# Experts of a mixture layer taken in pairs: a new order of units, one turning for two experts, and another ending for the last block

## The reference

```python
grp = jnp.argmax(g_logits, axis=-1)                 # one of 8 groups per token
top_val, top_idx = lax.top_k(e_logits, TOP_K)       # 2 of the 8 experts of that group
comb = jax.nn.softmax(top_val, axis=-1) * p_grp
# for each expert e, on its tokens:
h = jax.nn.silu(xb @ w1[e]) * (xb @ w3[e])          # 1024 -> 256, twice
y = h @ w2[e]                                       # 256 -> 1024
```

## Time and profile before

| | us |
|---|---|
| median of 3 runs | 1932.17 (1927.52 to 1934.03) |
| the profiled execution | 1933.65 |
| its span, first to last instruction | 1931.8 |
| PE busy | 1886.8 (98%) |
| DVE busy | 1437.1 (74%) |
| ACT busy | 1217.5 (63%) |

### The profile page before, as it was taken

One profiled execution on the slowest core, in us unless ns is written; L12 is line 12 of the kernel. 1 busy time (PEld: TensorE's weight loads), 2 busy tenths in 40 slices (PEclk: granted clock), 3 DMA queues, 4 the chain that ended last, 5 costly groups with the idle time before them and its releaser, 6 DMA issues.

```text
span 1931.8 us, 27066 instructions
## 1 busy us (share of the span) xinstructions
PE 1886.8 (98%) x9252; PEld 1571.1 (81%) x9252; DVE 1437.1 (74%) x1838; ACT 1217.5 (63%) x1538; POOL 162.3 (8%) x169
## 2 busy tenths in 40 slices
PE   9999999999999999999899999999999999999997
PEld 7978878888888888888789788788888888888885
DVE  5455544589899899999834655454898999999897
ACT  5455544357777777777634655434677777777775
POOL 1000000220010011010000000002200110110000
PEclk9999999999999999999999999999999999999999
DMA  5221193499999999999612222925999999999992
GB/s 173 71 66 45 52 236 114 185 332 395 391 383 365 386 385 366 381 389 373 217 66 59 66 65 74 239 90 183 371 394 384 385 367 376 393 370 375 386 381 99
DMA packets 158791, 503.54 MB, mean 261 GB/s; under 512 B 22410, under 2 KB 38794, under 8 KB 158704
## 3 DMA queue, kind: packets, MB, share of 16 engines
q1 hardware_dynamic: 146192, 459.70, 64.2%
q0 software_dynamic: 12512, 42.69, 7.6%
HBM read 490.18 MB, written 32.79 MB: 271 GB/s over the span
## 4 chain that ended last, share of the span: by engine, by line
PE 87%; DVE 6%; issue 2%; ACT 2%; DMA 2%; DVEq 0%; POOL 0%; SPq 0%; ACTq 0%; POOLq 0%
PE ps L1639 25%; PE ps L1641 25%; PE ps L1640 24%; PE ps L1882 3%; DVE wl L1115 2%; PE ps L1818 2%; PE ps L1868 2%; DMA yb<-yrows 2%; PE ps L2012 1%; PE ps L1973 1%; PE ps L1927 1%; PE ps L1985 1%; PE ps L1686 1%; DVE gb L1398 1%; DVE wl L1120 1%
## 5 line engine op out<-in xcount | busy, mean ns | idle before, releaser
L1115 DVE TENSOR_TENSOR wl<-raw,wh 128x2048 fp32r<-128x2048 f32 (+1 forms) x402 | 908.5, 2280 | 154.1 <-ACT wh L717 151.8
L717 ACT ACTIVATE wh<-raw 128x2048 fp32r<-128x2048 f32 (+1 forms) x406 | 754.3, 1884 | 64.6 <-PE ps L1641 64.0
L1639 PE MATMUL ps<-wh,xgh 128*128 128x512 f32 x1024 | 412.5, 403 | 0.2
L1641 PE MATMUL ps<-wh,xgl 128*128 128x512 f32 x1024 | 400.2, 391 | 0.0
L1640 PE MATMUL ps<-wl,xgh 128*128 128x512 f32 x1024 | 399.2, 390 | 0.0
L1641 PEld LDWEIGHTS ps<-wh,xgl 128*128 128x128 f32 x1024 | 192.2, 188 | 41.8
L1639 PEld LDWEIGHTS ps<-wh,xgh 128*128 128x128 f32 x1024 | 192.3, 188 | 37.7 <-issue 2.4
L1640 PEld LDWEIGHTS ps<-wl,xgh 128*128 128x128 f32 x1024 | 192.9, 188 | 36.1
L1639 PE MATMUL ps<-wh,hth 128*128 128x512 f32 x512 | 200.2, 391 | 3.1 <-DVE htl L1170 3.1
L1641 PE MATMUL ps<-wh,htl 128*128 128x512 f32 x512 | 200.0, 391 | 0.0
L1640 PE MATMUL ps<-wl,hth 128*128 128x512 f32 x512 | 199.3, 389 | 0.0
(11 more groups left out here) (320 smaller groups left out, 2658.6 us busy)
## 6 DMA issues: line engine op xcount, KB each, us to landing
raw<-in_w SPq DMA_DIRECT2D x512, 512.0 KB, 6.2
raw<-in_w SPq DMA_DIRECT2D x128, 1024.0 KB
raw<-in_w_gate SPq DMA_DIRECT2D x16, 1024.0 KB
xslots<-zrow POOLq DMA_DIRECT2D x2, 6240.0 KB, 36.2
raw<-in_w_out SPq DMA_DIRECT2D x8, 1024.0 KB
xg<-xslots POOLq DMA_DIRECT2D x14, 520.0 KB, 7.2
raw<-in_w_in SPq DMA_DIRECT2D x8, 800.0 KB
raw<-in_w_oa SPq DMA_DIRECT2D x4, 1024.0 KB
```

Of the source, the lines that this page charges most:

```text
L717: return nc.scalar.activation(dst, src, ACT.Copy)
L1115: return V.tensor_tensor(dst, src, hi.bitcast(F32), ALU.subtract)
L1639: MM(dst, lh, rh, start=first, stop=False)
L1641: return MM(dst, ll, rh, start=False, stop=last)
```

## The change

The unit list goes by pairs of experts: four up halves (both experts of a pair), then the two downs of the pair before. The pair's turn follows the second of these downs: four transposes in a row into the two halves of `ps2`, one copy of 512 columns on ACT, one on DVE. The two last downs of a block stand after the four first units of the next block, and the turn of experts 0 and 1 behind them (in block 0, which has no such tails, it stands after up 2 half 0). `y_first` and `y_second` move with the tail of expert 7, four units later than before. The transposes of the next block's rows move behind down 3; those of `sel` move from up 3 to up 4. The adds of earlier rows move to the first up halves of experts 4, 5, 6 and 7. In the last block the last units are up 6, up 6, up 7, down 4, up 7 (turn of 6), down 5 (turn of 7), down 6, down 7.

```diff
-    FIRST = [("up", 0, 0), ("up", 0, 1)]
-    for e in range(1, NE):
-        FIRST.append(("up", e, 0))
-        if e >= 2:
-            FIRST.append(("down", e - 2, 0))
-        FIRST.append(("up", e, 1))
-    FIRST.append(("down", NE - 2, 0))
-    LAST = [("tail", NE - 1, 0)]
-    NEXT = FIRST[:1] + LAST + FIRST[1:]
...
+    FIRST, NEXT = ups(0), ups(0) + downs(NE - 2, "tail")
+    for e in range(2, NE, 2):
+        FIRST += ups(e) + downs(e - 2)
+        NEXT += ups(e) + downs(e - 2)
+    ENDING = [("up", NE - 2, 0), ("up", NE - 2, 1), ("up", NE - 1, 0), ("down", NE - 4, 0), ("up", NE - 1, 1),
+              ("down", NE - 3, 0)] + downs(NE - 2)
+    ALONE = FIRST[:-6] + ENDING
+    FINAL = NEXT[:-6] + ENDING
+
+    def turned_after(u, units):
+
+        kind, e, half = u
+        if kind == "tail":
+            return [0, 1] if e == NE - 1 else []
+        if u == ("up", 2, 0):
+            return [0, 1] if units[4] == u else []
+        if units[-1] == ("down", NE - 1, 0) and e >= NE - 3:
+            return {("up", NE - 1, 1): [NE - 2], ("down", NE - 3, 0): [NE - 1]}.get(u, [])
+        return [e + 1, e + 2] if kind == "down" and e % 2 else []
...
-                act.wait_ge(S["used_m"], b * NU + (NU + 1))
+                act.wait_ge(S["used_m"], b * NU + (NU + 4))
...
-                        if kind == "up" and 3 <= e < 3 + NT and half == 0 and prepared and not prepare:
-                            earlier_rows(e - 3)
+                        if kind == "up" and e >= NE - NT and half == 0 and prepared and not prepare:
+                            earlier_rows(e - (NE - NT))
...
+                    def turn(experts):
+                        pe.wait_ge(S["hw_done"], b * NE + (experts[-1] + 1 + BASE["hw_done"]))
+                        pe.wait_ge(S["htl_done"], b * NE + (experts[0] + BASE["htl_done"]))
+                        for e in experts:
+                            for j in range(FE // P):
+                                at = (e % 2 * (FE // P) + j) * P
+                                last = nc.tensor.transpose(ps[2][:, at:at + P], hw[:, e % 2, j * P:(j + 1) * P],
+                                                           ident[:, :])
+                        last.then_inc(S["ht_ps"], len(experts))
...
-                        if u == ("up", NE - 3, 1) and prepare:
+                        if u == ("down", NE - 5, 0) and prepare:
                             rows_turned(b + 1)
```

More of the change, by code:

```diff
@@ L109, in user_before, with ups, downs @@
         return max((k for k in range(n) if at[k] == at[n]), default=None)
-    FIRST = [("up", 0, 0), ("up", 0, 1)]
-    for e in range(1, NE):
-        FIRST.append(("up", e, 0))
-        if e >= 2:
-            FIRST.append(("down", e - 2, 0))
-        FIRST.append(("up", e, 1))
-    FIRST.append(("down", NE - 2, 0))
-    LAST = [("tail", NE - 1, 0)]
-    NEXT = FIRST[:1] + LAST + FIRST[1:]
-    turn_after = {("up", 1, 0): 0}
-    for e in range(1, NE):
-        turn_after["down", e - 1, 0] = e
+    def ups(e):
+        return [("up", x, half) for x in (e, e + 1) for half in range(2)]
+    def downs(e, kind="down"):
+        return [(kind, x, 0) for x in (e, e + 1)]
+    FIRST, NEXT = ups(0), ups(0) + downs(NE - 2, "tail")
[15 more added lines that the diff above has]
+        return [e + 1, e + 2] if kind == "down" and e % 2 else []
     ctx = ExitStack()
@@ L338, in hybrid_trunk, with hth_of, ht_of @@
         block = ctx.enter_context(nc.Block())
+        def hth_of(experts, part=hth):
+            return part[:, experts[0] % 2:experts[0] % 2 + len(experts), :, :].rearrange("p e k t -> p (e k t)")
+        def ht_of(experts):
+            at = experts[0] % 2 * FE
+            return ps[2][:, at:at + len(experts) * FE]
         def dist_of(t):
@@ L534, in load_units @@
                         else:
-                            ex = (tail_g if kind == "tail" and i < 2 else g) * NE + e
+                            ex = (tail_g if kind == "tail" else g) * NE + e
                             src = w2[l].rearrange("e (k p) n -> e p k n", p=P)
@@ L540, in _ @@
                 load_units(FIRST, ND, 0, 0, None)
-                with sp.Fori(0, NG - 1) as r:
+                with sp.Fori(0, NG - 2) as r:
                     load_units(NEXT, ND + len(FIRST), r, r + 1, r)
-                load_units(LAST, ND + len(FIRST) + len(NEXT), NG - 2, NG - 1, NG - 1)
-                n_blocks = overflow(sp, lambda b, g: load_units(FIRST + LAST, ND, b, g, None))
+                load_units(FINAL, ND + len(FIRST), NG - 2, NG - 1, NG - 2)
+                n_blocks = overflow(sp, lambda b, g: load_units(ALONE, ND, b, g, None))
                 if l < L - 1:
@@ L1007, in step @@
                         kind, e, half = u
[L1008 to L1012, removed]
+                        turned = turned_after(u, units)
+                        if turned:
+                            act.wait_ge(S["ht_ps"], b * NE + (turned[-1] + 1))
+                            nc.scalar.activation(hth_of(turned), ht_of(turned), ACT.Copy
+                                                 ).then_inc(S["hth_done"], len(turned))
                         if kind == "up" and half == 1:
@@ L1024, in step @@
                             nc.scalar.activation(selt[:, :], ps[7][:, :], ACT.Copy).then_inc(S["selt_done"], 1)
-                        if kind == "tail" and n < n0 + 2:
+                        if u == ("tail", NE - 1, 0):
                             y_first(b - 1)
@@ L1573, in step @@
                         kind, e, half = u
[L1574 to L1578, removed]
+                        turned = turned_after(u, units)
+                        if turned:
+                            dve.wait_ge(S["hth_done"], b * NE + (turned[-1] + 1))
+                            lo_part(hth_of(turned, htl), ht_of(turned), hth_of(turned)
+                                    ).then_inc(S["htl_done"], len(turned))
                         if kind == "up" and half == 1:
@@ L2033, in pe_block @@
                         else:
-                            down(n0 + i, e, kind == "down" or i >= 2)
+                            down(n0 + i, e, kind == "down")
                         if u == ("up", 0, 0) and isinstance(b, int) and b == 0:
@@ L2041, in pe_block @@
                             last.then_inc(S["slot_ps"], 1)
-                        if u in turn_after:
-                            turn(turn_after[u])
-                        if u == ("up", NE - 3, 1) and prepare:
+                        if turned_after(u, units):
+                            turn(turned_after(u, units))
+                        if u == ("down", NE - 5, 0) and prepare:
                             rows_turned(b + 1)
-                        if u == ("up", 3, 0) and not prepare:
+                        if u == ("up", 4, 0) and not prepare:
                             pe.wait_ge(S["sel_made"], (b - (NG - 2)) * NT)
```

6 lines of the change are left out of this document (3 added, 3 removed).

## The result

Side by side on the same chips, the changed kernel takes 1936.24 us (median of 19 runs, 1932.03 to 1938.51) and the kernel before 1932.37 us (19 runs, 1925.38 to 1934.21): ratio 1.0021, 95% interval 1.0013 to 1.0028. That is 4 us more, inside the 0.3% that the prediction counts as no change, and 3 us above its 1933.1. The time fell into the range; the sum behind it was right in its large terms, and missed one that gains and two that cost.

The account below looks back on a forecast made before the run. PE was taken to be bound by its own matmuls, so only transposes and waits could change. Terms -4.6 - 0.6 + 3.2 + 2.9 = +0.9 us on the median 1932.2 gave 1933.1; range 1927 to 1942.

Parts of the forecast that it names:

- turns (and tail): PE's transposes: one going-in less per pair, 76 x 0.06 = -4.6 us; waits at block-end tails gone, -0.6.
- the loop's branch: PE at the loop's end: the branch's cost was taken to stay, so no gain was counted.
- block 0: Turn of 0 and 1 waits for DVE's `hw` of expert 1: +1.6 us per layer, +3.2 in all.
- last block, DVE's wait: Second add waits for its load, so PE waits before turns of 4 and 5 and of 7: +2.9 us for both layers.
- clock at a layer's end: PE's granted clock at the last turn and downs: forecast to stay 1.00, costing nothing.
- The loop's own branch stays: Loop end: the tail's loss goes, but the branch's own cost on PE remains after the change.
- the load's wait: Last block: DVE loses 3.1 us at the second add, waiting for its load of earlier rows.
- its first rival: Long wait before the turn of 7 lowers PE's clock: some +3 us per layer; 1939, or 1945 with late load; chance 0.24.
- The rival's other half, a late fourth load: Last block: the fourth add's load takes 7.8 us, so the turn of 7 comes 2.9 us later.
- Wrong if the clock falls at the end of a layer: A sign that would refute the forecast: granted clock below 1.00 at a layer's end.
- no steady block has idle PE: Steady blocks: any idle PE there would show the forecast wrong; they were to be 0.3 us shorter.
- the turn of 4 and 5 waits: Last block: PE loses about 1.1 us before this turn; the forecast is wrong if it never waits.

Follow-up runs that it names:

- The first edit: The changed kernel with the four adds of earlier rows moved to up 4 half 0, down 2, up 7 half 0 and down 5: 1929.46 us, ratio 0.9983.
- the second: The changed kernel with block 0's turn of experts 0 and 1 one unit later, after up 2 half 1: 1930.93 us, ratio 0.9999 to before.
- the two shifts: Never-executed waits move layer 1's code: 11 instructions on in the changed kernel, 1932.07 us; 235 on in the kernel before, 1936.76 us.

## Why the prediction was right, and where by luck

By its own steps, for both layers, in us of the profiled execution:

| step | predicted | measured | |
|---|---|---|---|
| turns (and tail) | -4.6 (-0.6) | about -5 | 14 blocks x (0.52 - 0.2), and six turns of the last blocks |
| the loop's branch | 0 | -2.4 | ten times |
| block 0 | +3.2 | +2.8 | 2 x 1.4 |
| last block, DVE's wait | +2.9 | +2.9 | +1.26 and +1.65 |
| clock at a layer's end | 0 | +1.6 | layer 0 alone |
| gap between the layers | 0 | +3.1 | the code's place |
| start of the kernel | 0 | -0.7 | scatter |

The rows of "measured" come to 2.3; the spans differ by 2.7.

- **The turns** were sized right, from three counts of transposes. The Trainium skill (TensorE: Matmul & The Clock Gate, Part 4: PE-mode transpose) has the access latency dominate such a transpose of about 275 ns. If each paid that in full, four would take 1.1 us and joining them would save nothing; here four take 0.49 us together.
- **"The loop's own branch stays" was wrong.** It is the one step of the walk through the units that failed; the clock, below, is the other failure inside the mixture. It was said without reading the row: the 0.35 at 608.49 depends on what stands before the branch, and behind four transposes nothing of it is left.
- **Block 0 and the last block** came out as walked, place by place and within 0.2 us, the load's wait too (2.87 for 3.1). Walking DVE's list with durations of the trace was enough, since the engines run in order. The first edit shows that the adds' distances are the cause (not the second add alone, see there), the second that block 0 is a cost of its own.
- **The clock.** The forecast said 1.00 throughout; its first rival said +3 per layer. It was 1.6, in one of two layers. Over the five profiles that keep the long wait the clock fell in four of ten layer ends; over the five with at most 1.02 us of idle PE there, in none of ten. So the rival's place and condition hold. But the length of the wait alone doesn't decide it: waits of 2.11 to 2.15 us stand on both sides, and what else decides stays open. Its price was put at nearly double, because the clock comes back before the two downs are through. The Trainium skill (TensorE: Matmul & The Clock Gate, Part 1: The HAM clock gate) states that idling lowers the clock; the trace agrees, and shows that 2.1 us do it at times. The rival's other half, a late fourth load, did not happen: that add shows no wait at 942.54.
- **The gap between the layers** stood in no case. The prediction read the 6.21 us "issue" of the earlier trace rows for the clock, and did not ask what the engine waited for. The branch alone would have made the forecast -1.5 instead of +0.9; the clock and the gap then bring 4.7. That the forecast time came within 0.2% is partly owed to omissions of both signs.

"Wrong if the clock falls at the end of a layer" was met in one layer; no steady block has idle PE, and the turn of 4 and 5 waits.

## What to carry to other kernels

When a reordering is costed, walk each in-order engine's list at the two ends of the loop, with the distance of every one-buffer load from its user: adds too close together for their loads cost 3.4 us per layer on an engine that doesn't use them, and the places of these adds and of one turn, set by hand, were worth 12 us, where the merging itself brings 5, or 7 with the loop's branch. When a difference stands in code that was not touched, look for the instruction queue among the DMAs: how the code lies behind a far jump is worth 3 us here and can be moved for nothing with instructions in a branch that isn't taken. Compare orders of work only after that, or the place of the code is taken for an effect of the order.

## What the runs showed of the hardware

- Code is fetched in packets of 16 KB (54 packets, 0.88 MB), and where it lies decides a wait. PE is idle 5.6 to 6.2 us at the jump over the unused block in the four kernels with one fetch in that stretch, and 9.0 to 9.5 us in the six with two. In these six a weight load stands alone, and its own matmul comes 3.4 to 3.8 us later. That a border between two fetches lies between them is inferred from this and from the two shifts.
- A taken branch of PE's loop shows nothing behind four transposes, 0.2 to 0.3 us behind two, and 0.3 to 0.4 behind a turn that has just waited.
- 2.1 us of idle PE were followed by the clock's 1.2 GHz level in four of ten cases, for some 1.6 us of time lost each time it could be read (7.34 and 7.35 us instead of 5.76 from the turn to the last down's end).
